# Strassen's seven products for the queries, keys and values of sparse attention heads, taken in pairs

## The reference, cut

```python
h = rms_norm(x, norm_g[l])
proj = h @ w_in[l]
...
qb = rotary(rms_norm(q_b.reshape(B, S, DSA_HEADS, DSA_HD), dsa_q_norm_g[l]), positions)
kb = rotary(rms_norm(k_b.reshape(B, S, DSA_HEADS, DSA_HD), dsa_k_norm_g[l]), positions)
vb = v_b.reshape(B, S, DSA_HEADS, DSA_HD)
...
y_b = dsa_attention(qb, kb, vb, qib, kib, wib).reshape(B, S, D_DSA) * jax.nn.silu(z_b)
...
g = jax.nn.sigmoid(gate.astype(jnp.float32)).astype(dt).reshape(B, S, N_BRANCH, D_MODEL)
merged = (g[:, :, 0] * (y_a @ w_branch[l, 0])
          + g[:, :, 1] * (y_b @ w_branch[l, 1])
          + g[:, :, 2] * (y_m @ w_branch[l, 2]))
x = x + merged @ w_out[l]
```

## Time and profile before

| | us |
|---|---|
| three runs | 976.05, 1627.19, 975.87 |
| median | 976.05 |
| span of the profiled execution | 974.9 |
| TensorE busy | 970.7 |
| VectorE busy | 649.9 |
| ScalarE busy | 518.5 |
| GpSimd busy | 246.0 |

### The profile page before, as it was taken

The page is one execution under the profiler, slowest core; times in us unless marked ns, Lnnn a source line. Parts: engine busy times, 40 slices in busy tenths (PEclk is TensorE's granted clock), DMA queues, the critical chain, the costliest instruction groups (busy, mean ns, idle before and its releaser), DMA issues.

```text
span 974.9 us, 13868 instructions
## 1 busy us (share of the span) xinstructions
PE 970.7 (100%) x4993; PEld 857.5 (88%) x4993; DVE 649.9 (67%) x1047; ACT 518.5 (53%) x790; POOL 246.0 (25%) x167
## 2 busy tenths in 40 slices
PE   9999999999999999999999999999999999999998
PEld 7888888898989989989898888898998989988887
DVE  6878987779565564653756443796776867735486
ACT  6977644445453453544447211776675857741351
POOL 0100822121011010010110800271622626106600
DMA  8624222112332322332322342707024050638412
GB/s 277 242 87 130 87 87 76 45 54 68 95 97 65 97 65 78 84 95 66 97 87 87 87 129 76 237 12 213 4 80 146 31 153 1 229 94 302 153 43 87
DMA packets 111622, 103.36 MB, mean 106 GB/s; under 512 B 4468, under 2 KB 95192, under 8 KB 111196
## 3 DMA queue, kind: packets, MB, share of 16 engines
q1 hardware_dynamic: 111564, 102.80, 33.5%
q10 hardware_dynamic: 16, 0.00, 0.0%
HBM read 98.59 MB, written 4.20 MB: 105 GB/s over the span
## 4 chain that ended last, share of the span: by engine, by line
PE 100%; POOL 0%; issue 0%; DVE 0%; POOLq 0%
PE proj L619 59%; PE proj L1064 9%; PE att L1091 7%; PE proj L1091 5%; PE att L1141 3%; PE proj L789 2%; PE att L946 2%; PE att L964 2%; PE att L886 1%; PE att L908 1%; PE proj L1021 1%; PE att L954 1%; PE att L935 1%; PE att L679 1%; PE att L1021 1%; PE proj L1141 1%
## 5 line engine op out<-in xcount | busy, mean ns | idle before, releaser
L1807 DVE TENSOR_TENSOR w_lo<-w_raw,w_hi 128x1536 fp32r<-128x1536 f32 (+1 forms) x58 | 124.0, 2138 | 134.8 <-ACT w_hi L1191 129.5
L1191 ACT ACTIVATE w_hi<-w_raw 128x1536 fp32r<-128x1536 f32 (+1 forms) x58 | 97.4, 1680 | 147.9 <-PE proj L619 147.7
L619 PE MATMUL proj<-hT_hi,w_hi 128*128 128x512 f32 x384 | 150.2, 391 | 0.0
L619 PE MATMUL proj<-hT_hi,w_lo 128*128 128x512 f32 x384 | 149.8, 390 | 0.0
L619 PE MATMUL proj<-hT_lo,w_hi 128*128 128x512 f32 x384 | 149.6, 390 | 0.0
L619 PE MATMUL proj<-w_hi,hT_hi 128*128 128x384 f32 (+1 forms) x280 | 96.7, 345 | 0.0
L619 PE MATMUL proj<-w_hi,hT_lo 128*128 128x384 f32 (+1 forms) x280 | 95.3, 340 | 0.0
L619 PE MATMUL proj<-w_lo,hT_hi 128*128 128x384 f32 (+1 forms) x280 | 95.1, 340 | 0.0
L619 PEld LDWEIGHTS proj<-hT_hi,w_lo 128*128 128x128 f32 x384 | 72.1, 188 | 15.2
L619 PEld LDWEIGHTS proj<-hT_lo,w_hi 128*128 128x128 f32 x384 | 72.1, 188 | 14.5
L619 PEld LDWEIGHTS proj<-hT_hi,w_hi 128*128 128x128 f32 x384 | 72.1, 188 | 14.5
(11 more groups left out here) (445 smaller groups left out, 2399.3 us busy)
## 6 DMA issues: line engine op xcount, KB each, us to landing
w_raw<-w_in_in SPq DMA_DIRECT2D x106, 256.0 KB, 3.2
w_raw<-w_in_in SPq DMA_DIRECT2D x32, 512.0 KB, 4.4
w_raw<-w_in_in SPq DMA_DIRECT2D x6, 1024.0 KB, 5.3
w_raw<-w_mem_kv_in SPq DMA_DIRECT2D x10, 512.0 KB, 7.2
yF<-x_in SPq DMA_DIRECT2D x8, 512.0 KB, 7.9
w_raw<-w_branch_in SPq DMA_DIRECT2D x16, 256.0 KB, 3.5
w_raw<-w_branch_in SPq DMA_DIRECT2D x4, 1024.0 KB, 6.4
w_raw<-w_branch_in SPq DMA_DIRECT2D x8, 512.0 KB, 5.5
```

Source lines behind the costliest of these rows:

```text
L619: ins = mm(ps, lhs[a](k, k0), rhs[b](k, k0), start=(first and k == 0 and j == 0), stop=(last and k == KH - 1 and j == 2))
L1191: A_(w_hi[:, kh, :, 0:n], w_raw[:, kh, :, 0:n], ACT.Copy).then_inc(w_hi_done, 1)
L1807: V.tensor_tensor(w_lo[:, kh, :, 0:n], w_raw[:, kh, :, 0:n], w_hi[:, kh, :, 0:n].bitcast(F32), ALU.subtract).then_inc(w_lo_done, 1)
```

## The change

The eight heads of B are taken as four pairs. Tokens are cut in two halves, the 1024 input rows in two halves, and the two heads are the two column halves: queries, keys and values of a pair are then one product of 2 x 2 blocks, done by Strassen's method in seven products (`b_product`, each 2 token blocks x 12 matmuls of 384 columns) in place of eight. The pair's first head is called r (number 2i), its second l (2i + 1). For it the change adds:

- four sums of blocks of h, made once by GpSimd in the M section (`token_blocks`) and split by ScalarE and VectorE (`bs_split`, `bs_low_of`);
- four weight sums per pair by GpSimd (`b_weight_sum`, 4 operations of 384 columns per row block): three early ones (`b_early_sums`, for the next pair) and a late one (`b_late_sum`);
- per pair 11 operands to be split into a ring of three places (`b_high(n)`, `b_low(n)`; numbers 0 to 6 are the seven products, 7 to 10 the halves of two f panels; number 11 and up here stand for the next pair's 0 and up; over all pairs the last pair's are 33 to 41);
- copies out of the banks (`b_save`, `b_last_copy`) and adds (`b_add`) by which the seven products become the two heads' raw queries, keys and values.

The 512-column work of a pair is two panels of three blocks (`f_panel`): z of one head and two blocks of gates of M or B; the sigmoids go to DRAM (`gate_evac`, `f_gate_stores`, `sig_kept`) and come back later. Attention of r is done by hooks in the same pair's panels, attention of l (the tail) between the products of the next pair. The last pair has four blocks in one panel. The gates' first panel stands alone ahead of the first pair (`start_gates`). y of M and of B also go to DRAM and come back (`ym_kept`, `yb_kept`), and the branch projections of M and B are four full panels after the last pair (`branch_panel`, `branch_merge`).

```diff
+PAIRS, B_OPS = B_HEADS // 2, 11
+B_SLOT = (0, 2, 1)
+B_RAW = "acabadcbadc"
...
+            def f_load(slot, i, j, kh):
+                if i == PAIRS - 1:
+                    b_load(slot, [(C_ZB + 2 * i * P, 2 * P)], kh)
+                else:
+                    q = 2 * i + j
+                    gate = C_GATE + 2 * D + 512 + 256 * q if q < 2 else C_GATE + D + 256 * (q - 2)
+                    b_load(slot, [(C_ZB + (2 * i + 1 - j) * P, P), (gate, 256)], kh)
+
+            def gate_store(index, stage):
+                sp.dma_start(sig_kept[index], sig[:, stage]).then_inc(gate_sent[stage], 16)
+
+            def f_gate_stores(i, j):
+                for b in (1, 2):
+                    sp.wait_ge(bank_empty[b], BF[2][b] + 2 * i + j + 1)
+                    gate_store(4 + 2 * (2 * i + j) + b - 1, b - 1)
...
+                    sp.wait_ge(op_low, n + 8)
+                    unit_load("b", i + 1)
+                    sp.wait_ge(op_low, n + 9)
+                    unit_load("a", i + 1)
+                    sp.wait_ge(op_low, n + 10)
...
+            sp.wait_ge(op_low, n + 9)
+            sp.wait_ge(yb_sent[0], SENT0 + 16 * (PAIRS - 1))
+            load(GB[0], [(wb[2], 0, 512)])
...
-            def b_turn_qk(h):
-                pe.wait_ge(b_rotated, h + 1)
-                if not (isinstance(h, int) and h == 0):
-                    pe.wait_ge(b_pcopied, h * 4)
+            def b_turn_qk(a):
+                pe.wait_ge(b_rotated, a + 1)
+                if a == 0:
+                    pe.wait_ge(m_y, 2 * M_HEADS)
+                elif a % 2:
+                    pe.wait_ge(b_masked, a * 4)
                 else:
...
-            def b_turn_p(h):
+            def b_turn_p(a):
+                if a % 2 == 0:
+                    pe.wait_ge(b_qcopied, a + 2)
+                    pe.wait_ge(b_kcopied, a + 2)
...
+            def b_product(i, m, lhs, to, start, before):
+                n = B_OPS * i + m
+                w = [b_op(op, n).rearrange("p (k n) -> p k n", k=KH) for op in (b_op_hi, b_op_lo)]
+                pe.wait_ge(op_low, n + 1)
...
+            def b_unit(i):
+                main, other = (banks[0], banks[1]), (banks[2], banks[3])
+                tail = 2 * i - 1
+                b_product(i, 0, h_block(0, 0), main, True,
+                          lambda t: (bank_empty[t], BF[2][t] + 2 * i) if i else (bank_empty[t], BS[2][t] + 1))
+                if i:
+                    b_score(tail)
+                b_product(i, 1, h_block(KH, 0), other, True,
+                          lambda t: ((bank_empty[2], BF[2][2] + 2 * i), (u_added, 6 * i))[t] if i else (bank_empty[2 + t], BS[2][2 + t] + 1))
+                if i == 0:
+                    pe.wait_ge(s_low, 3)
+                b_product(i, 2, h_sum(0), main, False, lambda t: (u_saved, 6 * i + t + 1))
+                if i:
+                    b_turn_p(tail)
+                b_product(i, 3, h_sum(1), main, False, lambda t: (u_saved, 6 * i + t + 3))
+                if i:
+                    b_values(tail)
+                b_product(i, 4, h_sum(2), other, True, lambda t: (u_added, 6 * i + t + 1))
+                if i == 0:
+                    pe.wait_ge(s_low, 4)
+                b_product(i, 5, h_sum(3), other, False, lambda t: (u_saved, 6 * i + t + 5))
+                b_product(i, 6, h_block(KH, HALF_T), main, False, lambda t: (u_added, 6 * i + t + 3))
+
...
+            for i in range(PAIRS):
+                b_unit(i)
+                r, l = 2 * i, 2 * i + 1
+                if i < PAIRS - 1:
+                    f_panel(i, 0, (0, P, 2 * P), {2: [lambda: b_turn_qk(r)], 4: [lambda: b_score(r)]})
+                    f_panel(i, 1, (0, P, 2 * P), {0: [lambda: b_turn_qk(l)], 1: [lambda: b_turn_p(r)], 3: [lambda: b_values(r)]})
                 else:
...
+                    f_panel(i, 0, (P, 0), {3: [lambda: b_turn_qk(r)]})
...
+            branch_panel(0, y_split(1), {1: [lambda: b_score(r)], 2: [lambda: b_turn_qk(l)], 4: [lambda: b_turn_p(r)],
+                                         6: [lambda: b_values(r)]})
+            branch_panel(1, None, {0: [lambda: b_score(l)], 3: [lambda: b_turn_p(l)], 5: [lambda: b_values(l)]})
...
+            def b_body(i):
...
+                b_high(n + 9)
+                b_qk_high(r)
+                b_high(n + 10)
+                z_evac(r)
+                gate_evac(i, 0)
+                b_exps(r)
+                b_high(n + 11)
+                b_qk_high(l)
+                b_probs_high(r)
+                b_high(n + 12)
+                z_evac(l)
+                b_values_high(l)
+                gate_evac(i, 1)
+
...
+            act.wait_ge(u_done, 2 * PRODUCTS * PAIRS)
+            split_hi(GB[0], 0, GB[1] + 1, 512)
+            b_qk_high(r)
+            z_evac(r)
+            z_evac(l)
+            act.wait_ge(proj_done[1], BF[2][1] + 2 * PAIRS - 1)
...
+            def b_body(i):
+                n, last = B_OPS * i, i == PAIRS - 1
+                tail, r, l = 2 * i - 1, 2 * i, 2 * i + 1
+                b_low(n + 2)
+                if i:
+                    b_maxes(tail)
+                b_low(n + 3)
+                b_add(i, 1, (banks[2], banks[3]), b_raw[:, 0:2], 1)
+                if i:
+                    b_scale_p(tail)
+                b_low(n + 4)
+                if i:
+                    b_probs(tail)
+                b_low(n + 5)
+                b_low(n + 6)
+                if i:
+                    b_finish(tail)
                 else:
...
+                    for _ in range(4):
                         top_round(2)
...
                     make_masks()
...
+                b_add(i, 3, (banks[0], banks[1]), b_fifth, 5)
+                b_low(n + 7)
+                b_add(i, 5, (banks[2], banks[3]), b_second, 3)
+                b_rotary(r)
+                b_low(n + 8)
+                b_values_low(r)
+                if last:
+                    return
+                b_low(n + 9)
+                b_qk_low(r)
+                b_rotary(l)
+                b_low(n + 10)
+                b_maxes(r)
+                b_scale_p(r)
+                b_low(n + 11)
+                b_qk_low(l)
+                b_probs(r)
+                b_low(n + 12)
+                b_finish(r)
+                b_values_low(l)
+
...
+            b_low(0)
+            m_rest(M_HEADS - 1)
+            bs_low_of(3, 4)
+            b_low(1)
+            for _ in range(4):
+                top_round(2)
+            for _ in range(4):
+                top_round(1)
...
+            r, l = B_HEADS - 2, B_HEADS - 1
+            for k in range(4):
+                ym_low(k)
+            split_lo(GB[0], 0, 512)
+            b_qk_low(r)
+            b_rotary(l)
             split_lo(GB[0], 1, 512)
...
+            b_maxes(r)
+            for k in range(4, KT):
+                ym_low(k)
+            b_qk_low(l)
+            b_scale_p(r)
+            b_probs(r)
...
+            def b_weight_sum(out, left, right, op):
+
+                for k in range(KH):
+                    at = slice(k * UNIT_N, (k + 1) * UNIT_N)
+                    ins = G.tensor_tensor(b_w[out][:, at], b_w[left][:, at], b_w[right][:, at], op)
+                ins.then_inc(t_done, 1)
...
+            def b_late_sum(i):
+                pool.wait_ge(t_done, 4 * i + 3)
+                pool.wait_ge(op_low, B_OPS * i + 3)
+                b_weight_sum("a", "d", "a", ALU.subtract)
```

895 lines of the change are left out of this document (586 added, 309 removed).

## The result

The changed kernel takes 1017.33 us (median of 4 runs, 1014.33 to 1018.63) against 976.25 us before; the ratio is 1.0414, with a 95% interval of 1.0395 to 1.0433. It is 4.1% slower; the forecast was 1000, 2.4% slower, with a range from 970 to 1021.

What follows compares the result with a forecast made beforehand. TensorE, busy 970.7 of 974.9 us, was taken as the bound; 974.9 - 16.7 + 21.6 (three pairs) + 9.3 (start of B) + 9.6 (end of B) = 998.7, plus 1.1 for the median, said as 1000 us, range 970 to 1021.

Steps and rivals of the forecast that it cites:

- TensorE's gain: Four pairs save 96 matmuls of 384 columns at 0.1735 us: 16.7 us off TensorE's work.
- Inside a pair: TensorE waits 3.7 at the transposes of l and 3.5 at b_turn_p(r): 7.2 us, in three pairs 21.6.
- the stretching: VectorE operations slowed beside GpSimd's squares and sums in a pair: +0.8 at b_rotary(r), +1.6 at b_rotary(l), +0.8 at low(10).
- The start of B: VectorE's splits, top rounds and masks delay TensorE in the first pair: 9.3 us, bounds 0 and 14.
- The end of B: Last pair: 5.6 before the first branch panel, 4.0 at the transposes of l; 9.6 us, bounds 5 and 14.
- The rival of the clock: Clock falls to half level in eight new waits, each such start costing about 3 us: 1024; chance 0.13.
- my signs of being wrong: TensorE without gaps in f_panel, a seam at the products, or a granted clock under 1.00.
- stay fed: Rival: TensorE never waits, as VectorE runs ahead; 959 us, chance 0.08.
- the floor: Rival: little contention, only 4.0 us lost per pair, and a start that VectorE absorbs; about 980, chance 0.25.
- The lock: Skill's exclusive port rule for VectorE and GpSimd: about 12 us more over three pairs; not used in the forecast.
- The DRAM traffic: Stores and reloads of y and gates, 15 MB over some 400 us: taken as nothing, bound 4 us.
- the rival that stores come late: Gate evacuations wait for their stage and panels for banks: 4 to 10 us more, 1008; chance 0.06.

Runs made afterwards that it cites:

- e13_best: e11_more with two places mended, in the last pair and the first pair (order of splits, low parts, top-k rounds, masks); 965.63 us, ratio 0.9885.
- e2_nosums: Changed kernel without GpSimd's weight sums of B, but for one operation of 2 columns each (computes something else); 1012.10 us, ratio 1.0366.
- e4_low10: Changed kernel with low(10) and the low part of r's values moved on VectorE behind the maxima of r; 1017.44 us, ratio 1.0429.
- e11_more: Changed kernel with reordered start of B, e6_pool's wait, moves inside a pair and seven more, including exp of r ahead of the third block's sigmoid; 977.85 us.
- e12_table: As e11_more, but with both sigmoids ahead of exp of r, as in the change; 981.88 us, ratio 1.0056.
- e6_pool: Changed kernel with GpSimd's sums of h for the A heads held until VectorE has split all of B's y; 1008.88 us, ratio 1.0326.
- e1_fill: Changed kernel with 11 or 18 extra 512-column matmuls into the unused fourth bank ahead of the transposes of l; 1021.98 us, ratio 1.0476.

## Why the prediction was right in sign and short in size

**TensorE's gain** of 16.7 was right: the 768 matmuls of 384 columns for B's queries, keys and values became 672, and in e13_best, whose waits sum to 5.5, the span is 963.3, against 958.2 forecast for a TensorE always fed. The change does what it says; its order costs 56.4 us, more than three times the gain.

**Inside a pair** the mechanism held and the size was 1.3 low: 8.8, 8.7 and 8.0 lost, forecast 7.2. The two waits stood where they were forecast, 4.0 and 2.1 in the second pair against 3.7 and 3.5; the second is the shorter as the slow transposes and matmuls ahead of it fill 1.5. The step that was mis-sized is the stretching. I took +0.8 from one operation under sums all through the earlier trace rows and counted four operations. Six were hit, each by 0.7 to 0.8 whatever its size, the one of four columns too: 1.5 in the rotary of r and 3.0 in that of l and low(10), 4.6 in place of 3.2. Six is also the number of GpSimd's operations beside them, two squares and four parts of a sum. The stretching also moved the transposes of r, where a wait of 0.7 came in the second and third pair that the forecast did not have.

What I had not seen is that two chains end at exp of r and so at `b_turn_p(r)`: VectorE's and, ready 2.1 us before it in the second pair, ScalarE's (third block, sigmoid, table load). I wrote that exp's table "is in, the load of 1.28 is done before the wait ends"; that was true for this order, and hid how little there was to win on VectorE alone. e2_nosums and e4_low10 showed it, and e11_more against e12_table prices exp's place at 4.0.

**The start of B**: 11.7 measured against 9.3; the waits before the third and seventh product were there (2.1 and 1.9 for 2.9 and 2.9), and before the transposes of r (2.7 for 2.0). One of 1.4 before the fourth product, for ScalarE's save behind high(4), was not in the working, nor the slow matmuls behind the first wait, 1.6. The fifth product, which I had named too, waited for nothing.

**The end of B**: about 9 against 9.6, but not where I put it, so that the sum fits is luck. Before the first branch panel I forecast 5.6, and 2.1 were measured. The load was right: low of its weights ended 21.2 after the sixth product, forecast 21.5. The step that failed is when TensorE comes there: 20.2 in place of 15.9. It had already lost 2.1 in the last pair, where the second half waits for low(41), 1.4 in slow matmuls behind this wait, and more in the slow transposes. I had low(41) in the chain of the load and overlooked that TensorE waits for it first. The wait was ended by ScalarE, whose SiLU of the last head's z reads the bank that the panel wants (L1756), 1 us behind the weights. The transposes of l waited 0.9 in place of 4.0, TensorE being late by then.

**Missing altogether** were 6.7 us in the third and fourth branch panel. GpSimd's sums of h for the A heads, four each of two kinds, start when B's last y is done. Before, one split of y ran beside them; now all eight splits of B's y stand there, and seven of them meet GpSimd. This is in the order of the change, and no term of the sum was for it: it is the largest term that the forecast lacked. e6_pool settles it with one wait. So the 17.3 us between forecast and median are: 6.7 here, 3.9 in the three pairs, 2.4 at the start of B, less 0.6 at its end, 3.3 of this execution's late start, and 1.6 by which the median is further above the span than before.

**The rival of the clock** came in half. It forecast 3 us for each new wait, 1024. A granted clock under 1.00 was among my signs of being wrong, and it came. The half clock stood behind eight of the ten rests of 2 us and more, not behind the one of 2.1 shown above, and in these eight stretches the matmuls of 384 and 512 columns lost 11 us to it. But each of these stretches is followed by a wait whose end VectorE or ScalarE sets. For the stretch behind the transposes of l e1_fill shows that it cost nothing; for the others that is read from the order and was not tried. e1_fill and e4_low10 show what the half clock costs where nothing follows, 1.6 to 1.7 each. By the rule of the Trainium skill (TensorE: Matmul & The Clock Gate, Part 1) the clock drops after idleness and comes back after steady work; the traces agree, with 0.50 behind 4.0 us of rest and 1.00 some 3 us later in the second pair, 6 us later in the third.

**The other rivals.** TensorE did not stay fed (959), and more than the floor was lost (980): 4.6 us of stretching in a pair.

**The lock.** The Trainium skill (SBUF — State Buffer, Terms) has VectorE and GpSimd hold their common ports for a whole instruction. I used the row of an A head and not this rule, which has the cost grow with the other engine's instruction. The traces side with the rule, in kind and in size. The 1.35 of the earlier trace rows by which I priced it holds GpSimd's own wait for VectorE. Without that a part of a sum takes 1.0 and a VectorE operation that meets it loses 0.7 to 0.8, and for GpSimd's 2.39 it is 2.2: in both sizes GpSimd's own time less 0.2, and the same for 4 columns as for 512. The two engines take turns, so one GpSimd operation holds up one VectorE operation: that is why six were hit, and why L2548 was not. Not every GpSimd operation holds the ports that long: beside its power (L3054, 8 columns, 2.02 us) the products of the rotary (L2540), two SBUF inputs each, took their usual 0.69:

```profile
371.46 2.50 DVE L2540 TENSOR_TENSOR arena<-arena,tabs 128x512 f32<-128x512 f32 x4
...
371.63 2.02 POOL L3054 TENSOR_TENSOR small<-small,minus_half 128x8 f32<-128x8 f32 x1 [8.17 <-DVE small L2532]
```

**The DRAM traffic** at nothing fits: no wait of TensorE in the profile is put down to a store, and e13_best keeps all of it. It was not tried apart. No row speaks for the rival that stores come late (1008).

## What to carry to other kernels

Where an engine is fed without a gap, as TensorE was here, an algorithm that takes work from it pays only if the chain that feeds it still ends in time. Add up that chain at each place where the fed engine asks, for each other engine alone, since shortening one uncovers the next. Sums by GpSimd belong where VectorE waits: the same sums cost 6.7 us in one place and nothing 14 us later. Price them by GpSimd's time with nothing beside it, once for each of its operations. Waits of the matrix engine are to be judged together: the slow stretch behind a long one was free where a later wait took it up, and was paid in full behind the last.

## What was not expected of the hardware

An operation of VectorE with four columns (L2547) went from 0.16 to 0.97 us beside GpSimd, so the loss does not go by the instruction's own length; the one of four columns lost as much as that of 1536. And a single move could make the kernel slower than no move: filling a rest of 4 us with matmuls cost 4.7 us in total, 1.7 of it in the second pair, where the rest that remained came last.
